# Turning q and k by VectorE's 32x32 block transposes instead of TensorE's

## The reference

```python
h = rms_norm(x, g_mix)
proj = h @ w_in                      # q, k: 256 x 1024 each (4 heads of 256)
q, k, v, r, lr, ... = split(proj)
log_a = log_sigmoid(lr @ w_gate_up + b_gate) / 16      # one value per token and channel
# per head: S_t = diag(a_t) S_{t-1} + k_t^T v_t ;  o_t = (q_t / 16) S_t
```

## Time and profile before

| | |
|---|---|
| median of 3 runs | 2216.22 us (2216.21 to 2216.39) |
| profiled execution, its own time | 2216.83 us |
| its span (first to last instruction) | 2215.0 us |
| PE busy | 2203.9 us (99%) |
| DVE busy | 1382.4 us (62%) |
| ACT busy | 990.9 us (45%) |
| POOL busy | 225.6 us (10%) |
| mean granted TensorE clock | 0.999 |

### The profile page before, as it was taken

How to read it: one execution, slowest core, us unless ns; L and a number is a source line. 1 busy time by engine, 2 the same in 40 slices (tenths; PEclk the granted TensorE clock), 3 DMA queues, 4 the chain that set the end, 5 groups by cost and what they waited for, 6 DMA issues and landing times.

```text
span 2215.0 us, 24339 instructions
## 1 busy us (share of the span) xinstructions
PE 2203.9 (99%) x10186; PEld 1832.5 (83%) x10186; DVE 1382.4 (62%) x1301; ACT 990.9 (45%) x934; POOL 225.6 (10%) x253
## 2 busy tenths in 40 slices
PE   9999999999999999999999999999999999999998
PEld 8888888888888888888888888888888888888886
DVE  6577645545555545556855864864775677786755
ACT  7464654333333433344433433433444455555542
POOL 1023010000000000000100000000100122253201
PEclk9999999999999999999999999999999999999999
DMA  9555566677877776655655556566556755656663
GB/s 320 189 172 170 163 189 196 209 218 219 241 230 226 218 210 198 228 190 172 208 190 190 194 197 197 172 209 193 190 194 203 245 186 190 195 167 182 229 229 115
DMA packets 217100, 444.88 MB, mean 201 GB/s; under 512 B 9316, under 2 KB 10484, under 8 KB 216096
## 3 DMA queue, kind: packets, MB, share of 16 engines
q1 hardware_dynamic: 206976, 411.07, 57.0%
q0 software_dynamic: 9728, 32.18, 6.1%
q10 hardware_dynamic: 288, 0.10, 0.0%
HBM read 427.08 MB, written 12.06 MB: 198 GB/s over the span
## 4 chain that ended last, share of the span: by engine, by line
PE 99%; DVE 0%; POOL 0%; POOLq 0%; ACT 0%; issue 0%
PE acc L1421 32%; PE acc L1422 31%; PE acc L1423 31%; PE side L1431 1%; PE side L1509 1%; PE side L1445 1%; PE side L1495 1%; PE side L1481 1%; PE acc L1436 0%; PE side L1466 0%; PE side L1465 0%; PE side L1464 0%; PE side L1530 0%; PE side L1531 0%; POOL X L661 0%; PE side L1552 0%
## 5 line engine op out<-in xcount | busy, mean ns | idle before, releaser
L963 DVE TENSOR_TENSOR wlo<-raw,whi 128x2048 fp32r<-128x2048 f32 x380 | 893.5, 2352 | 638.2 <-ACT whi L678 637.6
L678 ACT ACTIVATE whi<-raw 128x2048 fp32r<-128x2048 f32 x380 | 727.6, 1915 | 748.6 <-PE acc L1423 731.1
L1421 PE MATMUL acc<-whi,setA_lo 128*128 128x512 f32 x1792 | 700.3, 391 | 0.0
L1423 PE MATMUL acc<-whi,setA_hi 128*128 128x512 f32 x1792 | 697.6, 389 | 0.0
L1422 PE MATMUL acc<-wlo,setA_hi 128*128 128x512 f32 x1792 | 697.6, 389 | 0.0
L1421 PE MATMUL acc<-whi,setB_lo 128*128 128x512 f32 x1280 | 501.9, 392 | 0.0
L1422 PE MATMUL acc<-wlo,setB_hi 128*128 128x512 f32 x1280 | 498.7, 390 | 0.0
L1423 PE MATMUL acc<-whi,setB_hi 128*128 128x512 f32 x1280 | 498.3, 389 | 0.0
L1423 PEld LDWEIGHTS acc<-whi,setA_hi 128*128 128x128 f32 x1792 | 336.6, 188 | 69.8
L1421 PEld LDWEIGHTS acc<-whi,setA_lo 128*128 128x128 f32 x1792 | 336.8, 188 | 69.2 <-DVE wlo L963 0.3
L1422 PEld LDWEIGHTS acc<-wlo,setA_hi 128*128 128x128 f32 x1792 | 336.7, 188 | 68.8
(11 more groups left out here) (208 smaller groups left out, 1019.4 us busy)
## 6 DMA issues: line engine op xcount, KB each, us to landing
raw<-in_w_in SPq DMA_DIRECT2D x188, 1024.0 KB, 5.3
raw<-in_w_ffn_up SPq DMA_DIRECT2D x64, 1024.0 KB, 5.3
raw<-in_w_ffn_down SPq DMA_DIRECT2D x64, 1024.0 KB, 5.1
raw<-in_w_gla_out SPq DMA_DIRECT2D x16, 1024.0 KB, 5.1
raw<-in_w_conv_out SPq DMA_DIRECT2D x16, 1024.0 KB, 5.1
raw<-in_w_o SPq DMA_DIRECT2D x16, 1024.0 KB, 5.1
raw<-in_w_out SPq DMA_DIRECT2D x16, 1024.0 KB, 5.2
t_scratch<-t5v POOLq DMA_DIRECT2D x8, 512.0 KB, 7.2
```

What stands on the lines that cost most here:

```text
L678: e.activation(whi[r][:, :, :], raw[r][:, :, :], ACT.Copy).then_inc(s_hi, 1)
L963: e.tensor_tensor(wlo[r][:, :, :], raw[r][:, :, :], asf(whi[r][:, :, :]), ALU.subtract).then_inc(s_lo, 1)
L1421: e.matmul(o, xl, whi[r][:, k, :], start=kk == 0, stop=False)
L1423: f = e.matmul(o, xh, whi[r][:, k, :], start=False, stop=kk == 15)
```

## The change

q and k are no longer turned by TensorE and copied by ScalarE. The jobs `turn_qk` become `flip` and `flip_rest`: VectorE's block transposes write `qT` and `kT` directly. The counter of flips (`FN`) numbers all flipped units in order, since q and k now come before the `up` units. The factor 1/16, which ScalarE's copy of q had carried, moves to the k side of the level products, where a tensor_tensor becomes a scalar_tensor_tensor. The diff, cut:

```diff
-LATER = {"q": ("turn_qk",), "k": ("turn_qk",), ...
+LATER = {"q": ("flip", "flip_rest"), "k": ("flip", "flip_rest"), ...

             if kind == "cc":
                 return evacuated(TMPS[n] + 2)
-            if kind == "up":
-                return s_fl, 16 * j + 16
+            if TMPS[n] in FN:
+                return s_fl, 16 * FN[TMPS[n]] + 16

-            def copies(u, dst, scale):
-                for b in range(2):
-                    n = SN["turn", u, b]
-                    e.wait_ge(*full("turn", u, b))
-                    e.activation(dst[:, 2 * b:2 * b + 2, :], two(side[n % 4][:, :]), ACT.Copy,
-                                 scale=scale).then_inc(s_read[n % 4], 1)
...
-                    for b in range(2):
-                        e.wait_ge(*seen("turn", UI["k", 1], b))
+                    e.wait_ge(s_fl, 16 * FN[UI["k", 1]] + 16)
...
-                e.tensor_tensor(qv[:, :, 0:w], kt[:, :, 0:w], dd[:, :, 0:w], ALU.mult).then_inc(s_kq, 1)
+                e.scalar_tensor_tensor(out=qv[:, :, 0:w], in0=kt[:, :, 0:w], scalar=0.0625, in1=dd[:, :, 0:w], op0=ALU.mult,
+                                       op1=ALU.mult).then_inc(s_kq, 1)
...
             def flip(u, half):
-                j = UNITS[u][1]
-                k = 4 * (j % 4)
-                if half == 0:
+                kind, j = UNITS[u]
+                if half == 0 and kind == "up":
                     e.wait_ge(*set_free(u))
                     e.wait_ge(s_pq, j + 1)
+                elif half == 0:
+                    e.wait_ge(*evacuated(u))
+                k = 4 * (j % 4)
+                src = tmp_of(u)[:, :, :].rearrange("p t (k r n) -> p t k r n", k=4, r=4)
+                dst = {"q": qT, "k": kT, "up": A_raw}[kind][:, k:k + 4, :].rearrange("p k (t q n) -> p t k q n", t=2, q=4)
                 for q in (0, 1) if half == 0 else (2, 3):
                     for r in range(4):
-                        e.transpose(dst[:, :, :, q, :], src[:, :, :, r, :]).then_inc(s_fl, 1)
+                        e.transpose(dst[32 * r:32 * r + 32, :, :, q, :],
+                                    src[32 * q:32 * q + 32, :, :, r, :]).then_inc(s_fl, 1)
...
-                    elif job == "flip_split":
+                    elif job in ("flip_rest", "flip_split"):
                         flip(a, 1)
```

More of the change, by code:

```diff
@@ L22 @@
 NS = 4 * len(UNITS)
-LATER = {"q": ("turn_qk",), "k": ("turn_qk",), "r": ("turn_r",), "cx": ("shift", "none", "conv0", "conv1"), "cb": ("turn_cb",),
+LATER = {"q": ("flip", "flip_rest"), "k": ("flip", "flip_rest"), "r": ("turn_r",), "cx": ("shift", "none", "conv0", "conv1"), "cb": ("turn_cb",),
          "yb": ("turn_yb",), "wo": ("turn_wo",), "up": ("flip", "flip_split"), "q2": ("none", "turn_qk2"),
@@ L148 @@
 TN = {}
+FN = {}
 def buckets():
@@ L171, in number @@
             tmps += tmp_use(job, a)
+            if job == "flip":
+                FN[a] = len(FN)
     for n, key in enumerate(order):
@@ L865, in scalar @@
                         e.activation(ro[:, :, :], ro[:, :, :], ACT.Sqrt).then_inc(s_rq, 1)
-                    elif job == "turn_qk":
-                        kind, j = UNITS[a]
-                        copies(a, (qT if kind == "q" else kT)[:, 4 * j:4 * j + 4, :], 0.0625 if kind == "q" else 1.0)
                     elif job == "turn_r":
@@ L889, in scalar @@
                         k = 4 * (j % 4)
-                        e.wait_ge(s_fl, 16 * j + 16)
+                        e.wait_ge(s_fl, 16 * FN[a] + 16)
                         e.activation(A_hi[:, k:k + 4, :], A_raw[:, k:k + 4, :], ACT.Copy).then_inc(s_fh, 1)
@@ L1172, in flip @@
             def flip(u, half):
-                j = UNITS[u][1]
-                k = 4 * (j % 4)
-                if half == 0:
+                kind, j = UNITS[u]
+                if half == 0 and kind == "up":
                     e.wait_ge(*set_free(u))
                     e.wait_ge(s_pq, j + 1)
+                elif half == 0:
[3 more added lines that the diff above has]
+                dst = {"q": qT, "k": kT, "up": A_raw}[kind][:, k:k + 4, :].rearrange("p k (t q n) -> p t k q n", t=2, q=4)
                 for q in (0, 1) if half == 0 else (2, 3):
                     for r in range(4):
-                        src = tmp_of(u)[32 * q:32 * q + 32, :, :].rearrange("p t (k r n) -> p t k r n", k=4, r=4)
-                        dst = A_raw[32 * r:32 * r + 32, k:k + 4, :].rearrange("p k (t q n) -> p t k q n", t=2, q=4)
-                        e.transpose(dst[:, :, :, q, :], src[:, :, :, r, :]).then_inc(s_fl, 1)
+                        e.transpose(dst[32 * r:32 * r + 32, :, :, q, :],
+                                    src[32 * q:32 * q + 32, :, :, r, :]).then_inc(s_fl, 1)
             def finish(t):
```

## The result

The change made the kernel slower: 2225.36 us (2224.26 to 2227.54, five runs) against 2216.39 us (2216.21 to 2216.98). The ratio is 1.0041, with a 95% interval of 1.0028 to 1.0054, or +9.0 us: small, but clear of the noise. The forecast was 2223.0 in a range of 2219.0 to 2226.5. The profiled execution is the slowest of the five, 2227.54 us for a span of 2225.7.

A forecast was written before the change was run, and what follows sets the result against it. PE, busy 2203.9 of 2215.0 us, was taken to bound the kernel. Its gain and the stalls, -3.5 + 2.8 + 4.2 + 0.85 + 0.8 + 1.65 = +6.8 us, took 2216.22 to 2223.0 us; range 2219.0 to 2226.5.

The forecast's parts named there:

- What bounds: Whole kernel: only PE's own row moves the end; PE is busy 2203.9 of 2215.0 us, other engines are hidden.
- PE's gain, -3.5 us: PE loses four turns of eight transposes, 0.88 us each, 3.5 us in all, the whole gain.
- The copies and the factor at nothing: ScalarE's four dropped pairs of copies bring no gain; VectorE's k product as scalar_tensor_tensor costs nothing, at most 8 x 0.01 us.
- A flip at 0.465 us: Each of VectorE's 64 block transposes of 32x256 takes 0.465 us, as in the feed-forward stage; 29.8 us in all.
- The cheap bound of 0.40: Lower price of a flip, 0.40 us, from the cheapest row of 256 elements; change then +2.8 us, 2219.0 us.
- Stalls of 2.8 and 4.2 us at steps 10 and 11: PE waits 2.8 us before step 10 and 4.2 us before step 11 for weight low halves behind q's flips.
- 0.85, 0.8 and 1.65 us for k: Behind k's flips PE stalls 0.85 us before step 15, 0.8 before the gate matmuls, 1.65 before step 22.
- The sum, +6.8 us: All terms together, PE's gain against five stalls: +6.8 us, so 2223.0 us, 0.31% slower.
- rival A: PE's clock falls to 1.2 GHz in the stall before step 11, costing 2 us more: 2225.0 us; chance 0.13.
- B: Rival: VectorE absorbs the flips and only PE's gain is left, 2212.7 us; chance 0.07.
- C: Rival: mostly absorbed, cheap flips or slack in the log-sigmoid chain; 2214 to 2220.6 us, likeliest 2219; chance 0.13.
- D: Rival: weight loads slip after three are released within 5 us, delaying step 14; about 2226 us; chance 0.05.

The follow-up runs named there:

- spread: Changed kernel with all 64 flips kept, but a few at a time behind the low half in steps 8 to 16 and 19; 2213.04 us, ratio 0.9984.
- factor_only: Kernel before with only the factor 1/16 moved to the k side, all turns still on TensorE; 2216.58 us, ratio 1.000.
- after_again: The changed kernel run once more, unaltered, on the same chip as filled_again; 2225.49 us, ratio 1.0041.
- k_only: Changed kernel with q given back to TensorE, so only k is flipped on VectorE; 2218.31 us, ratio 1.0008.
- k1_late: Changed kernel with only the flips of k's second unit moved, three to step 16 and thirteen to step 19; 2222.84 us, ratio 1.0027.
- filled_again: Changed kernel with twelve unused small matmuls ahead of step 10 and seventeen ahead of step 11, on after_again's chip; 2224.64 us, ratio 1.0036.
- q_only: Changed kernel with k given back to TensorE, so only q is flipped on VectorE; 2224.1 us, ratio 1.0031.
- pe_filled_both: Changed kernel with twelve unused small matmuls ahead of step 10 and seventeen ahead of step 11; 2224.69 us, ratio 1.0036.

## Why the prediction was right, and where it was short

**What bounds.** Right. PE's row decides, and every wait of steps 10 to 22 shows up in the end: in both traces of the changed kernel no distance changed from step 22 on.

**PE's gain, -3.5 us.** Right. `spread` shows it alone, 2213.04 for 2216.68, or -3.6.

**The copies and the factor at nothing.** Right; `factor_only` shows the second. That ScalarE's copies are no gain was only argued, but `spread`, which has no copies either, leaves only 0.1 us that they could explain.

**A flip at 0.465 us.** Right: 3.70 and 7.44 us. The cheap bound of 0.40 does not occur. (The terms printed for it, +3.1 - 0.9 + 0.5, make 2.7 and not 2.8; nothing hangs on it.)

**Stalls of 2.8 and 4.2 us at steps 10 and 11.** Right in place and size. In `after_again` step 12 begins at 79.38, forecast 79.3. In the profiled run the first was 3.5, since VectorE's queue started 0.73 us later there. I took its start from one execution, and the start varies with the first loads.

**0.85, 0.8 and 1.65 us for k.** Right: 0.8, 1.0 and 1.65, shown by `k_only` and, for the last two, by `k1_late`.

**The sum, +6.8 us.** `after_again`, where no fall of the clock counts, is +7.16 at step 26. By the table, the 0.36 that are missing come in up to step 12 (0.1), between 12 and 16 (0.1) and between 16 and 19 (0.2), and nothing from there on. A small term that I left out explains part of it: a step that begins with a wait is some 0.13 us longer (5.58 for 5.44), since its first matmuls start 0.34 us apart and not 0.227. It counts at steps 11 and 15. At step 22 it is no loss, since the kernel before restarts there too (5.59 us), and at step 10 of `after_again` it vanishes in the next wait. The rest is the gate's stall, 1.0 us for 0.8.

**The clock, rival A at 0.13.** This is the step that was off, and by the prediction's own sign: a granted clock below 1.00 near 74 us was named as what would show it wrong, and the profiled run has 0.50 there. I held the fall for unlikely, since the stall of 4.2 us was at the edge of the 3.8 us of idleness seen at the end, and the other stalls were shorter. That edge was one execution's. In the two traces of the changed kernel the clock falls after 2.8 us and, in the shorter of the two stalls, after 2.1 us (63.3, idle since 61.17). Behind the last matmul it falls after 2.2 us in `k1_late` (2210.95 to 2213.18) and after 4.7 in `filled_again` (2213.53 to 2218.25). All ten timed executions of the changed kernel have a mean clock of 0.997, where the kernel before has 0.998 or 0.999. The rule of the Trainium skill that I weighed (TensorE: Matmul & The Clock Gate, "HAM oscillation — how this bites in real kernels"), that waits between bursts of matmuls put the array to half rate, is what these traces show. The price I took, 2 us, was of the right size only for a fall that meets the second stall (2.6 and 1.6 us); in the first it is nothing, which the prediction did not consider. Its price for a whole step at half rate, 5.4 us, does not follow from its own spacings either: 24 x (0.43 - 0.227) is 4.9.

**What is left.** Against the kernel before the change cost 9.0 us, 2.2 more than the sum. The filled kernels, with the clock at 1.00, still cost 8.0. So by the medians some 1 us of the 2.2 is the clock, a difference that is not clear of the runs' spread. The missing terms above are 0.4. For the rest, some 0.8, the traces name two things that differ from one execution to the next. VectorE's queue starts early or late: `wlo(9)` starts at 50.92 in `q_only` and at 52.38 in `k1_late`, and I took its start from one execution. And PE has a late wait in some, as the 0.94 us in `filled_again`. How they share in the median is not shown. That the median, 2225.4, lies so near rival A's 2225.0 is luck: A put the whole excess on the clock.

**Rivals B, C and D** fell. The flips were not absorbed, none was cheap, and the load for step 14 was no wait: step 14 begins 5.44 us after step 13.

## What to carry to other kernels

Work moved to an engine that is 62% busy costs nothing only where its idle time lies. Ask what stands behind it in that engine's queue, and how far ahead of its user that is: here the same 64 instructions made the kernel 9 us slower in one order and 3.6 us faster in another. Look for the places where the engine waits for a chain that the work does not lengthen (here 6.25 us beside ScalarE's log-sigmoid), and put it there. When TensorE waits for several microseconds, price the fall of its clock as well, and ask whether the step that then runs at half rate is one that somebody waits for. The idle time before a fall in one trace is no threshold: here it was anything from 2.1 to 4.7 us.

## What the runs showed of the hardware

The granted clock fell to 0.50 after 2.8 us of idleness in one run of the changed kernel (at 73.64, with another wait of 3.36 us before) and after 2.1 us in the other (at 63.3), where no wait had come before. In `q_only` and `k1_late` it fell 0.2 us and 1.0 us after matmuls had begun again, behind waits of 2.24 and 3.30 us; in `k_only` waits of up to 1.5 us brought no fall. Behind the last matmul it fell after 2.2 to 4.7 us. So one execution gives no threshold: the same wait can pass once and meet a fall the next time. In the changed kernel's profiled run it came back at 80.47, some 5.7 us after matmuls had begun again. In `filled_again` and `pe_filled_both`, small matmuls in the stalls kept it at 1.00. A fall in the first of two stalls cost nothing: step 10 was longer, and PE idled 1.12 us before step 11 in place of 3.90. VectorE's block transposes took the same time for each source and target here, 0.465 us for eight 32x32 blocks, and a scalar_tensor_tensor took what a tensor_tensor takes, 1217 ns for 1215 on 1024 elements in each of the eight levels, from rows of 128 elements down to rows of one.
